# Ten slots in each ring of gathered rows of a decoder block with expert retrieval, and the buffers made smaller for them

## The reference

```python
x += W_out[concat(MLA heads, RG-LRU groups, differential attention)](W_in rmsnorm(x))
x += memory cross-attention(rmsnorm(x), rmsnorm(mem))
x += PEER(rmsnorm(x))
out = rmsnorm(x)
# MLA scores of head h (4 heads, 64 plain + 32 turned features):
s1 = (einsum('bqhd,bkhd->bhqk', q_nope, k_nope) + einsum('bqhr,bkr->bhqk', q_rope, k_rope)) * mla_scale
# PEER, per block of 128 tokens: 8 heads x 16 chosen experts of 16384
act = gelu(einsum('td,thkd->thk', xt, u[et]))
y   = einsum('thk,thkd->td', gt * act, v[et])
```

## Time and profile before

| | |
|---|---|
| median of 3 runs | 3508.47 us (3501.45, 3508.47, 3508.81) |
| profiled execution | 3502.22 us, its span 3500.1 us |
| mean granted TensorE clock | 0.940 |
| PE busy, share of the span | 2942.9 us, 84% |
| DVE busy | 2341.0 us, 67% |
| ACT busy | 814.6 us, 23% |
| POOL busy | 2008.2 us, 57% |
| moved by DMA | 1346.12 MB, 391 GB/s from HBM over the span |

### The profile page before, as it was taken

How to read it: one execution, slowest core, us unless ns; L and a number is a source line. 1 busy time by engine, 2 the same in 40 slices (tenths; PEclk the granted TensorE clock), 3 DMA queues, 4 the chain that set the end, 5 groups by cost and what they waited for, 6 DMA issues and landing times.

```text
span 3500.1 us, 34723 instructions
## 1 busy us (share of the span) xinstructions
PE 2942.9 (84%) x10960; PEld 1660.0 (47%) x10960; DVE 2341.0 (67%) x5884; ACT 814.6 (23%) x1924; POOL 2008.2 (57%) x2085
## 2 busy tenths in 40 slices
PE   7786898888997899888987799888998789976777
PEld 6465355533554355444554445544554445522222
DVE  6229756886578765887477855786648866596554
ACT  3111421133111422133211332114221232211111
POOL 1003765666565664666555655666547655577775
PEclk9897999999999999999999999999999999998999
DMA  7787999999999999999999999999999999999998
GB/s 275 259 299 266 409 409 409 408 409 402 409 402 408 399 405 403 407 409 390 405 409 408 397 351 409 409 408 370 354 409 409 409 346 350 390 404 410 409 409 339
DMA packets 387256, 1346.12 MB, mean 385 GB/s; under 512 B 41793, under 2 KB 44865, under 8 KB 386433
## 3 DMA queue, kind: packets, MB, share of 16 engines
q0 software_dynamic: 294912, 1073.87, 78.0%
q1 hardware_dynamic: 91008, 265.83, 20.1%
q10 hardware_dynamic: 1152, 4.19, 0.3%
HBM read 1334.03 MB, written 35.39 MB: 391 GB/s over the span
## 4 chain that ended last, share of the span: by engine, by line
PE 43%; DMA 25%; DVE 14%; POOL 9%; issue 6%; ACT 3%; SPq 0%; DVEq 0%; ACTq 0%; POOLq 0%
PE ps_sum L1212 19%; DMA rows<-in_peer_u,ids_u 9%; PE ps_p L979 7%; DMA rows<-in_peer_v,ids_v 6%; DMA rows<-in_peer_v,ids_u 5%; POOL rows L802 5%; PE ps_s L1127 5%; POOL rows L792 4%; DVE rows L1986 4%; DMA w_ring<-packed 2%; PE ps_s L1065 2%; PE ps_p L1073 2%; DVE feat_b L1873 1%; PE ps_p L1047 1%; DVE feat_b L1869 1%
## 5 line engine op out<-in xcount | busy, mean ns | idle before, releaser
L1212 PE MATMUL ps_sum<-rows,diag 128*128 128x512 f32 x3584 | 1748.0, 631 | 271.9 <-DMA rows<-in_peer_v,ids_v 129.2
L1986 DVE CUSTOM_DVE_ANT_0 rows<-h_cur,rows 128x1024 f32<-128x1024 f32 x1024 | 1228.1, 1220 | 539.7 <-DMA rows<-in_peer_u,ids_u 527.0
L792 POOL DMA_INDIRECT rows<-in_peer_u,ids_u x1024 | 1005.4, 982 | 720.7 <-issue 498.8
L1212 PEld LDWEIGHTS ps_sum<-rows,diag 128*128 128x128 f32 x3584 | 684.1, 201 | 1166.4 <-issue 1047.8
L802 POOL DMA_INDIRECT rows<-in_peer_v,ids_v x512 | 493.5, 964 | 452.2 <-PE ps_sum L1212 295.6
L802 POOL DMA_INDIRECT rows<-in_peer_v,ids_u x512 | 494.4, 966 | 267.8 <-issue 127.3
L1466 ACT ACTIVATE diag<-ident,acts 128x128 f32<-128x128 f32 x896 | 327.4, 394 | 1057.4 <-PE ps_sum L1212 757.5
L979 PE MATMUL ps_p<-hT,w_ring 128*128 128x128 f32 x2944 | 367.8, 286 | 36.1 <-DMA w_ring<-packed 18.0
L979 PEld LDWEIGHTS ps_p<-hT,w_ring 128*128 128x128 f32 x2944 | 362.0, 202 | 68.6 <-issue 42.3
L1772 DVE CUSTOM_DVE_ANT_0 e<-ps_s,bias_t 128x256 f32<-128x256 f32 (+6 forms) x96 | 74.2, 773 | 177.5 <-PE ps_s L1065 70.6
L2007 DVE SCALAR_TENSOR_TENSOR x_cur<-rows,acts,x_cur 128x1024 f32<-128x1024 f32 x128 | 164.0, 1282 | 13.4 <-DMA rows<-in_peer_v,ids_v 13.4
(11 more groups left out here) (280 smaller groups left out, 2325.7 us busy)
## 6 DMA issues: line engine op xcount, KB each, us to landing
w_ring<-packed SPq DMA_DIRECT2D x343, 512.0 KB, 7.7
w_ring<-in_wstream SPq DMA_DIRECT2D x65, 512.0 KB, 5.3
packed<-in_wstream SPq DMA_DIRECT2D x49, 512.0 KB, 7.9
rows<-in_peer_u,ids_u POOLq DMA_INDIRECT x1024, 13.3
rows<-in_peer_v,ids_u POOLq DMA_INDIRECT x512, 10.7
rows<-in_peer_v,ids_v POOLq DMA_INDIRECT x512, 15.4
bias_rows<-rows SPq DMA_DIRECT2D x5, 1024.0 KB, 12.8
bias_t<-in_x SPq DMA_DIRECT2D x8, 512.0 KB, 6.2
```

The costliest lines, as they stand in the source:

```text
L792: pool.indirect_dma_start(u_rows[:, j % G_RING, :], None, peer_u, bass.IndirectOffsetOnAxis(ap=ids_u[:, j:j + 1], axis=0)).then_inc(u_land ...
L1212: ins = pe.matmul(ps_sum[:, c * 512:(c + 1) * 512], diag[:, n % 4, :], v_rows[:, j % G_RING, c * 512:(c + 1) * 512], start=(n == 0), stop= ...
L1986: dve.tensor_tensor_reduce(row, h_cur[:, :], row, 1.0, 0.0, ALU.mult, ALU.add, dots[:, p:p + 1]).then_inc(u_used, 1)
```

## The change

Both rings get 10 slots (`U_RING`, `V_RING`), 20 rows of 4 KB per partition in place of 16. A row's slot is now counted over all blocks, `(b * 128 + j) % 10`, and POOL's waits are written out for it. The 16 KB per partition come from smaller buffers:

- `k_mla` becomes `k_nope`, two heads' plain key features in one tile of 128 partitions, and `k_turned`, the turned features once (each group of 512 keys in another 32 partitions). A span's scores are two products that add up in PSUM: one over 64 partitions, one over 32.
- The queries are stored to match: `q_nope_t` (two ACT copies of two heads in place of one of four) and `q_turned`, which ACT copies once or twice to the partitions of the key groups (`q_spread`, in its `gates` stage); PE waits for that before the first scores.
- `wgate` has no zeros: 16 products of 64x64 in place of 8 of 128x128, loaded by two DMAs of 128 KB each.
- `ffn_row` and `gain_row` are gone. The two gains are held in 8 partitions (4 KB each), and PE spreads them over 128 partitions into `ps_s` when they are needed, by 8 products each (`spread`): the ffn gain once per block after the key scores (in `later_norm`, in the last block directly after them), the final gain for blocks 2 and later right after `mla_up`, behind a wait for ACT's copy of `ps_up`, and once in the tail. DVE reads `ps_s` at the same two places. PE waits before its next use of `ps_s` (`handed` in `latents`, `fin_made` in `mla`).
- `mla_up` makes k with two products of two heads.

```diff
-G_RING = 8
+U_RING = 10
+V_RING = 10
-SUM_SLOTS = G_RING - G_RING // SHARE
+SUM_SLOTS = 7
+ADD_SLOTS = 1
-        wgate = sb("wgate", [P, 2, LT, P])
+        wgate = sb("wgate", [P, 2, LT, LRU_G])
-        k_mla = sb("k_mla", [NOPE + ROPE, MLA_H, SEQ])
+        k_nope = sb("k_nope", [P, MLA_H // 2, SEQ])
+        k_turned = sb("k_turned", [P, HALF])
+        def row_slot(b, j, ring):
+            return (b * EXPERTS + j) % ring
...
+            def gather_v(b, j):
+                slot = row_slot(b, j, V_RING)
+                before = b * EXPERTS + j - V_RING
+                if before >= 0:
+                    added = before // SHARE + (1 if on_vector(before % EXPERTS) else 0)
+                    if on_vector(before % EXPERTS):
+                        pool.wait_ge(v_added, ADD_SLOTS + added)
+                    else:
+                        pool.wait_ge(v_used, SUM_SLOTS + before + 1 - added)
...
+            def spread(line, signal):
+                for kt in range(KT):
+                    one = bc(ident[96:96 + KT, 96 + kt:97 + kt], [KT, P])
+                    ins = pe.matmul(ps_s[:, kt * P:(kt + 1) * P], one, line, start=True, stop=True)
+                ins.then_inc(signal, 1)
+            def spread_ffn(b):
+                if isinstance(b, int) and b == 0:
+                    pe.wait_ge(consts_in, 112)
+                pe.wait_ge(k_out, 2 * b + 2)
+                spread(ffn_line, ffn_spread)
+            def spread_gain(b):
+                pe.wait_ge(gain_landed, 16)
+                pe.wait_ge(kv_out, 2 * b + 2)
+                pe.wait_ge(lat_n, b + 1)
+                spread(gain_line, gain_spread)
+            def later_norm(b):
+                spread_ffn(b)
+                turn_scaled(b + 1)
+            def last_scores(b):
+                peer_scores(b)
+                spread_ffn(b)
+            def later_up(b):
+                mla_up(b)
+                spread_gain(b)
...
-                        ins = pe.matmul(ps_p[a][:, i * P:(i + 1) * P], wgate[:, a, i, :], lru_x[:, i, :], start=True, stop=True)
+                        for h in (0, LRU_G):
+                            ins = pe.matmul(ps_p[a][h:h + LRU_G, i * P:(i + 1) * P], wgate[h:h + LRU_G, a, i, :],
+                                            lru_x[h:h + LRU_G, i, :], start=True, stop=True)
...
-                        ins = pe.matmul(ps_s[:, c0:c1], q_mla[0:NOPE + ROPE, n, :], k_mla[:, n, c0:c1], start=True, stop=True)
+                        r = NOPE * (n % 2)
+                        pe.matmul(ps_s[:, c0:c1], q_nope_t[r:r + NOPE, n // 2, :], k_nope[r:r + NOPE, n // 2, c0:c1],
+                                  start=True, stop=False, skip_group_check=True)
+                        r = ROPE * (c0 // HALF)
+                        ins = pe.matmul(ps_s[:, c0:c1], q_turned[r:r + ROPE, n, :], k_turned[r:r + ROPE, 0:c1 - c0],
+                                        start=False, stop=True, skip_group_check=True)
...
+                    pe.wait_ge(q_spread, b + 1)
+                    ge(pe, fin_made, b - 1)
...
+                for g in range((key_tiles(b) + 3) // 4):
+                    ins = copy(q_turned[g * ROPE:(g + 1) * ROPE, :, :], q_turned[NOPE:NOPE + ROPE, :, :])
+                ins.then_inc(q_spread, 1)
...
+                dve.wait_ge(ffn_spread, b + 1)
+                dve.scalar_tensor_tensor(h_cur[:, :], x_next[:, :], small[:, 105:106], ps_s[:, :], ALU.mult, ALU.mult)\
...
-                dve.wait_ge(gain_landed, 16)
-                dve.scalar_tensor_tensor(x_cur[:, :], x_cur[:, :], out_stat[:, 2:3], gain_row[:, :], ALU.mult, ALU.mult)\
+                dve.wait_ge(gain_spread, min(bp, NB - 2) + 1)
+                dve.scalar_tensor_tensor(x_cur[:, :], x_cur[:, :], out_stat[:, 2:3], ps_s[:, :], ALU.mult, ALU.mult)\
```

More of the change, by code:

```diff
@@ L545, in row_of, with row_landings @@
             return (bp, None) if isinstance(bp, int) and bp == 0 else (bp - 1, j + EXPERTS)
+        def row_slot(b, j, ring):
+            return (b * EXPERTS + j) % ring
+        def row_landings(b, j, ring):
+            return 16 * ((b * EXPERTS + j) // ring + 1)
         def ends_block(bp, p, at):
@@ L1016, in mla_up @@
                 pe.wait_ge(proj_out[4], b + 1)
-                for h in range(MLA_H):
-                    ins = pe.matmul(ps_p[0][0:NOPE, h * P:(h + 1) * P], wukv[:, 0, h * NOPE:(h + 1) * NOPE], latent_n[:, 2, :],
+                for i in range(MLA_H // 2):
+                    ins = pe.matmul(ps_p[0][:, i * P:(i + 1) * P], wukv[:, 0, i * P:(i + 1) * P], latent_n[:, 2, :],
                                     start=True, stop=True)
@@ L1239, in _ @@
             for pace.body, (first, last, wide[0]) in enumerate(LOOPS):
+                if first == 2:
+                    front["mla_up"] = later_up
+                if first == NB - 1:
+                    front["peer_scores"] = last_scores
                 with pe.Fori(first, last) as b:
@@ L1243, in _ @@
             pace.start(NB - 1)
+            pace.to(SUM_LAG - 1)
+            pe.wait_ge(handed, NB)
+            spread(gain_line, gain_spread)
             pace.to(END)
@@ L1982, in multiply_row @@
             def multiply_row(bp, p):
[L1984 to L1985 removed]
+                slot = row_slot(bp, p, U_RING)
+                dve.wait_ge(u_landed[slot], row_landings(bp, p, U_RING))
+                row = u_rows[:, slot, :]
                 dve.tensor_tensor_reduce(row, h_cur[:, :], row, 1.0, 0.0, ALU.mult, ALU.add, dots[:, p:p + 1]).then_inc(u_used, 1)
```

106 lines of the change are left out of this document (53 added, 53 removed).

## The result

The changed kernel takes 3547.88 us (median; 3545.06 to 3551.28), the kernel before on the same chip 3504.96: ratio 1.013, 95% interval 1.0118 to 1.0142. It is slower by 1.3%, above the top of the predicted range (3534). Its profiled execution took 3546.71 us, the span 3544.9, at a mean granted clock of 0.932 in place of 0.940.

A forecast was written before the change was run, and what follows sets the result against it. Retrieval was taken as bound by DMA bytes, with PE setting the pace in the attention holes. Terms +13.1 - 2.4 - 0.8 - 6 + 0.7 = +4.6 gave 3506.8, or 3513 us on the median's scale; range 3490 to 3534.

The forecast's parts named there:

- Scores in two products: Attention scores, blocks 2 to 7: second product costs 1.77 us per 1024 keys again, each shape change 0.14; 4.3 to 9.9 per block.
- a wait that hides part of each first head: First head's scores in blocks 4 to 7: PE's wait of about 0.6 us hides that much, -2.4 us in all.
- The ring's relief: Two more slots per ring: 5.1 us off the hole of each of six blocks, 30.7 at most, and 6 at the start.
- Block 7's end: Ffn gain after block 7's key scores: +3.2 us in the 5.4 hole, -4 from earlier rows, together -0.8.
- The prologue: Before retrieval: first block's scores cost 2.6 us, 0.78 MB less loading gives at most 1.9; sum +0.7.
- Gates and final gain: Sixteen gate products and the final gain behind `mla_up`: covered by PE's 5.5 us wait for DVE, so 0.
- Side by side: Rival, faster: odd heads' second score products run beside the first, giving back 14.6 us: 3498; chance 0.12.
- PE late to the attention: Rival, slower: final gain and gates delay PE 4.7 us per block before the scores, 19 us: 3532; chance 0.19.
- Relief twice: Rival, faster: deeper rings also remove stops in the second half of blocks 4 to 7, 20 us more: 3493; chance 0.12.
- Slots not filled: Rival, slower: POOL hardly gets ahead, the two added slots stay empty and the whole relief goes: 3550; chance 0.05.
- the rival in which the rings do nothing: Rival: the parts that cost are covered, the added slots give nothing, and the change does not show: 3508; chance 0.05.

## Why the prediction was wrong

**The step that failed** is "Scores in two products": it priced each product and each change of shape at the length that they have at TensorE's full clock, and had the clock only in its last sentence, as something that would make the prediction wrong. The products are as long as priced while the clock is up (4.2 us for a head in block 7; 1.77 + 1.77 + 0.7 were forecast). But the clock then drops to the 1.2 GHz level for the second head and what follows it, for a part of the head in block 4 (3.71 us for 2.99) and nearly all of it in blocks 5 to 7 (6.37 for 3.41, 7.21 for 3.85, 8.06 for 4.27). The price per product came from rows at which the clock stays up, the differential scores of the earlier trace rows: the reading was right, and it did not hold at the place where it was used.

From the runs the sum comes out as follows. One product with ten slots does not fit in SBUF; by the slots' worth it would take about 3493.2 - 15.5 = 3478 us, which is an estimate. The second product's columns, at 128 partitions, bring it to 3500.0: +22, against 29.2 + 0.9 - 2.4 = 27.7 in the forecast. The changes of shape are 0.7 us per head with two spans, 0.35 to 0.42 with one, some 14 to 16 us, which agrees with the forecast's 14.6. That makes about 3515. The changed kernel measured 3545.5 and 3547.9. The remaining 30 to 33 us are put down to the low clock, for which the sum had no term. That share is found by subtraction, from a start (3478) that is an estimate; it lies between the 11 and the 33 that the clock costs with 64 and 32 partitions. The -2.4 us for a wait that hides part of each first head was not tried alone.

**The ring's relief** was right as a sum: 34.6 us against 36.7. That the two lie so close is partly luck. Between the profiled executions with eight and with ten slots the holes differ by 5.2 us at the start (6 forecast), some 5 in block 2, nothing to 1 in blocks 3 and 4, and 6.1, 4.1 and 6.2 in blocks 5 to 7 (5.1 each forecast); the 9.5 at block 7's end, for which the forecast had 4 beside the 36.7, make up for blocks 3 and 4. It was not enough: forecast -0.8 to +4.8 per block, measured -2.8 and -1.6 in blocks 2 and 3 (better by 2.0 and 1.7), +15.1, +13.5, +17.2, +14.6 in blocks 4 to 7.

**Block 7's end** was undersized: -0.8 forecast, -4.9 measured. Both of its terms were real: with eight slots the hole is 4.1 us wider than before (3.2 forecast), with ten it is gone.

**The prologue.** The first gather comes 2.6 us earlier (+0.7 forecast). The second trace of the changed kernel has it at 286.53, 0.5 us earlier, so a term of this size can't be judged by one execution.

**Gates and final gain** at nothing: right for the gates by their own run. The final gain was not run alone; with everything but slots and scores at +4.3 us (1.4 to 7.7), and 4.1 in the hole at block 7's end, what it costs can't be told from nothing.

**The rivals.** Side by side: it happens, but not where it was looked for. The fourth head's plain product (partitions 64 to 127) and turned one (0 to 31) still start 1.05 us apart. Products of one shape in other partitions do overlap: the turned ones of two spans when they follow each other (1.13 us for two), and the gates' pairs. The sentence of the Trainium skill (TensorEngine Tiling (Array Packing), Key Properties) on tiles that work in parallel agrees with those two, and its sentence on the drain at a change of mode with the odd heads. PE late to the attention (3532): with the gain and the gates as changed, and one product, eight slots take 3508.7, where this rival would have up to 19 us more than the kernel before; and the loss lies in the attention, not ahead of it. Relief twice: it would be 20 us more than the 36.7 forecast, and 34.6 were measured. Slots not filled has the nearest time, 3550, and the wrong mechanism: the 34.6 us exclude it, and with it the rival in which the rings do nothing.

What stays open: whether alternating shapes have an effect on the clock beyond their few partitions (11 us of the 26, about the interval), and what about a head's place decides that few partitions lower the clock there and not in the differential scores.

## What to carry to other kernels

A product cut into pieces with fewer partitions costs its columns again, and here also TensorE's clock, for itself and for the full-height work behind it. A price per product taken from rows at one place holds at another only if the clock does. Where PE sets the pace, price such an edit at both levels of the clock, and try first the order that puts pieces of one shape, in different partitions, next to each other: here that alone gave back 31 of 43 us. A buffer that pays with PE time only at one place can be refused alone: nine slots with the scores in one product take 3493.2 us, a ratio of 0.9968 (0.9952 to 0.9984) to the kernel before. With the gates in either form that is the fastest version that computes the reference.

## What was not expected of the hardware

- The granted clock falls at a wait of 1.64 us with PE busy for the whole of 13 us before (7.99 of 8, 5.00 of 5), when the products are over 64 or 32 partitions. It shows even with one product per span over 64 (3.66 us in place of 1.98). Over 128 no second head in blocks 4 to 7 is slow. Over 96 some are: 3.03 us in place of 1.98 in block 7 with eight slots, 2.78 in place of 1.77 in block 6 with the gates as before.
- Behind longer waits it is often down with full-height products too. In the version with the gates as before, the 8 gate products over 128 partitions take 2.81 to 3.25 us behind three waits of 2.42 to 2.48 us for DVE and the usual 2.05 behind a fourth of 2.47 and two of 0.73; in the kernel before the waits there are 0.53 to 1.29 us, and all six take 2.05.
- Two products over 32 partitions each, in different partitions and writing different spans of `ps_s`, take 1.13 us together, one of them 1.05 to 1.12.
- A float32 product of 32 columns over 32 partitions, between products over 64, puts its successor's start off by 0.33 us, its two changes of shape included: about a third of what 512 columns take.
- The final gain's products, over 8 partitions, have the low clock behind them too, in five of six blocks of the changed kernel (three rows in 7.11 to 8.07 us, against 5.31 in the earlier trace rows; 5.42 in block 5), and in five of six of the version with 128 partitions twice, which takes 3500.0 us. What that costs was not tried alone; all the parts beside slots and scores cost 4.3 us together:

```profile
2802.30 2.69 PE L1023 MATMUL ps_s<-wuq,ident 8*128 8x128 f32 x16 [1.12 <-issue]
2804.92 8.07 PE L1273 MATMUL ps_sum<-rows,diag 128*128 128x512 f32 x12
```

- One chip of those used grants the kernel before a clock of 0.90 to 0.91, and it takes 3709 us there, 5.8% more than the others.
